# PEER's rows of u: turned by VectorE in 32x32 squares and multiplied as plain fp32, on one core

## What is computed

```python
def peer_ffn(h, q_w, sub_keys, u_tab, v_tab):      # h: 256 x 1024, u_tab and v_tab: 16384 x 1024
    q = (t @ q_w).reshape(n, PEER_H, 2, PEER_DQ // 2)
    s = jnp.einsum('thpd,hpnd->thpn', q, sub_keys)
    s1, i1 = lax.top_k(s[:, :, 0], PEER_TOPK); s2, i2 = lax.top_k(s[:, :, 1], PEER_TOPK)
    ...                                            # the 16 best of the 16 x 16 sums, for each of 8 heads
    gates = jax.nn.softmax(top_s, axis=-1)
    act = jax.nn.gelu(jnp.einsum('chkd,cd->chk', u_tab[i_c], x_c))
    return jnp.einsum('chk,chkd->cd', g_c * act, v_tab[i_c])
```

## Time and profile before

| what | value |
|---|---|
| median of 3 runs | 2324.53 us (2319.58 to 2325.33) |
| the profiled execution: its own time | 2319.86 us |
| its span | 2318.1 us |
| granted clock over the span | 0.966 of full speed |
| busy over the span | PE 2145.5 us (93%), DVE 1409.6 us (61%), ACT 1016.8 us (44%), POOL 186.9 us (8%) |
| HBM | 330.58 MB read, 143 GB/s over the span |

### The profile page before, as it was taken

One profiled execution on the slowest core, in us unless ns is written; L12 is line 12 of the kernel. 1 busy time (PEld: TensorE's weight loads), 2 busy tenths in 40 slices (PEclk: granted clock), 3 DMA queues, 4 the chain that ended last, 5 costly groups with the idle time before them and its releaser, 6 DMA issues.

```text
span 2318.1 us, 37450 instructions
## 1 busy us (share of the span) xinstructions
PE 2145.5 (93%) x14407; PEld 1931.0 (83%) x14407; DVE 1409.6 (61%) x2315; ACT 1016.8 (44%) x1870; POOL 186.9 (8%) x217
## 2 busy tenths in 40 slices
PE   6999899878899999789999699999999999999997
PEld 6876788778788889778888599999999999777775
DVE  5435777677676752154434628997666654666665
ACT  4443443458553343233333424443444444555554
POOL 2101000001000000300000000000223341000000
PEclk9999999999999999879999899999999999999998
DMA  7543566734657743300001333343333335555553
GB/s 254 184 172 110 190 218 220 245 117 160 221 166 267 252 158 131 83 1 1 1 1 37 109 111 128 128 137 119 115 113 114 115 119 175 189 190 190 190 190 136
DMA packets 157432, 333.74 MB, mean 144 GB/s; under 512 B 17382, under 2 KB 69340, under 8 KB 157160
## 3 DMA queue, kind: packets, MB, share of 16 engines
q1 hardware_dynamic: 153896, 321.18, 41.0%
q0 software_dynamic: 3392, 10.52, 1.3%
HBM read 330.58 MB, written 1.08 MB: 143 GB/s over the span
## 4 chain that ended last, share of the span: by engine, by line
PE 73%; DVE 12%; PEld 7%; ACT 3%; issue 3%; SPq 1%; DMA 1%; PEldq 1%; DVEq 0%; ACTq 0%
PE psum L2130 18%; PE psum L2131 17%; PE psum L2132 17%; PE psum L2652 4%; PE psum L2699 2%; PEld psum L2130 2%; PEld psum L2131 2%; PEld psum L2132 2%; DVE weights_lo L1493 2%; PE psum L2542 2%; PE psum L2548 2%; DVE u_lo L2080 1%; PE psum L2523 1%; ACT weights_hi L1037 1%; PE psum L2428 1%
## 5 line engine op out<-in xcount | busy, mean ns | idle before, releaser
L1493 DVE TENSOR_TENSOR weights_lo<-weights,weights_hi 128x1024 fp32r<-128x1024 f32 (+2 forms) x336 | 345.3, 1085 | 260.4 <-ACT weights_hi L1037 255.3
L2130 PE MATMUL psum<-input_hi,weights_hi 128*128 128x256 f32 x1288 | 370.9, 288 | 19.0 <-DVE weights_lo L1493 6.1
L1037 ACT ACTIVATE weights_hi<-weights 128x1024 fp32r<-128x1024 f32 (+2 forms) x336 | 289.2, 931 | 178.7 <-PEq L2177 117.5
L2131 PE MATMUL psum<-input_lo,weights_hi 128*128 128x256 f32 x1288 | 367.1, 285 | 0.0
L2132 PE MATMUL psum<-input_hi,weights_lo 128*128 128x256 f32 x1288 | 366.9, 285 | 0.0
L2130 PE MATMUL psum<-input_hi,u_hi 128*128 128x256 f32 x1024 | 299.8, 293 | 0.0
L2132 PE MATMUL psum<-input_hi,u_lo 128*128 128x256 f32 x1024 | 289.3, 283 | 0.0
L2131 PE MATMUL psum<-input_lo,u_hi 128*128 128x256 f32 x1024 | 289.2, 282 | 0.0
L2130 PEld LDWEIGHTS psum<-input_hi,weights_hi 128*128 128x128 f32 x1288 | 250.0, 194 | 34.6 <-issue 32.7
L2080 DVE TENSOR_TENSOR u_lo<-psum,u_hi 128x512 fp32r<-128x512 f32 x256 | 164.8, 686 | 167.4 <-ACT u_hi L1419 165.9
L2131 PEld LDWEIGHTS psum<-input_lo,weights_hi 128*128 128x128 f32 x1288 | 250.0, 194 | 0.0
(11 more groups left out here) (376 smaller groups left out, 4001.4 us busy)
## 6 DMA issues: line engine op xcount, KB each, us to landing
u_rows<-in_peer_u_dram SPq DMA_DIRECT2D x128, 512.0 KB, 3.4
weights<-in_ffn_w_in_dram SPq DMA_DIRECT2D x44, 1024.0 KB, 7.3
v_rows_even<-in_peer_v_dram SPq DMA_DIRECT2D x64, 512.0 KB, 3.5
v_rows_odd<-in_peer_v_dram SPq DMA_DIRECT2D x64, 512.0 KB, 3.4
weights<-in_ret_w_in_dram SPq DMA_DIRECT2D x24, 1024.0 KB, 7.3
ada_rows_in<-in_ada_w_dram SPq DMA_DIRECT2D x24, 1024.0 KB, 5.2
weights<-in_ffn_w_out_dram SPq DMA_DIRECT2D x44, 512.0 KB, 6.5
weights<-in_lru_w_in_dram SPq DMA_DIRECT2D x12, 1024.0 KB, 6.3
```

The costliest lines, as they stand in the source:

```text
L1037: nc.scalar.activation(whi[:, r, at_], wraw[:, r, at_], ACT.Copy).then_inc(s_whi[r], 1)
L1493: ins = nc.vector.tensor_tensor(wlo[:, r, at_], wraw[:, r, at_], whi[:, r, at_].bitcast(F32), ALU.subtract)
L2130: nc.tensor.matmul(o, ah, bh, start=start, stop=False)
L2131: nc.tensor.matmul(o, ah, bl, start=False, stop=False)
```

## The change

For blocks 0 to 112 ("plain" blocks; PARTED is 113) the rows of u are no longer split. DVE transposes them in 32x32 squares from SBUF to SBUF into one of four buffers, and PE makes 8 plain fp32 products of 256 columns with an input that is not split either (`input_t`, HT, made once by POOL as the sum of hi and lo). A transpose in squares stays inside groups of 32 partitions, so the order of the contraction is changed to fit: row 256a + 32k + j of the contraction goes to partition 32a + j of chunk k. That reaches the load of u (4 DMAs of 32 rows, 1 KB to a partition), the load of the query weights (8 DMAs of 256 KB for a slot instead of 2 of 1 MB), and the second operation of `modulate`, which writes in that order. Blocks 113 to 127 are still split, from the turned rows in SBUF, with one ACT and one DVE operation of 128x1024. The one-hot rows are made by one DVE comparison of 128x1024, and ACT multiplies in the gates with four operations of 128x128.

```diff
+PARTED = GROUP_FIRST + GROUPS
+def plain_buffer(j):
+    return j % 4
+def parted(j):
+    return (j - PARTED) // 2 + 1
...
+        HT = Region("u's hi parts, before", low.at, 8 * KB).take("input_t", [P, KT, S])
+        UF2 = Region("u's lo parts, before", low.at, 8 * KB).take("u_turned_more", [P, 2, KT, P])
+        UT = Region("idle rows", rows_at, 8 * KB).take("u_turned", [P, 2, KT, P])
+        UF = [UT[:, 0], UT[:, 1], UF2[:, 0], UF2[:, 1]]
...
             def load_u(j, i=0):
-                    sp.wait_ge(s_ut[b], i * 2 + 2 * (j // 2))
-                sp.dma_start(UR[:, b, :], u_tab[bass.ds(i * 256 + j * P, P), :]).then_inc(s_ur[b], 16)
+                    sp.wait_ge(s_ut[b], i + j // 2)
+                for c in range(4):
+                    four = u_tab[bass.ds(i * 256 + j * P + c * 32, 32), :].rearrange("e (a k) -> a e k", a=4)
+                    sp.dma_start(UR[:, b, c * 256:(c + 1) * 256], four).then_inc(s_ur[b], 16)
...
+            for j in (2, 3):
+                r, use = slot(SLOTS["peer_q"] + j)
+                pool.wait_ge(s_wlo[r], use + 1)
+            for h in range(2):
+                half = slice(4 * h, 4 * h + 4)
+                nc.gpsimd.tensor_tensor(HT[:, half, :], HH[:, half, :].bitcast(F32), HL[:, half, :].bitcast(F32), ALU.add)\
+                    .then_inc(s_ht, 1)
...
             def u_high(j):
+                if j < PARTED:
+                    return
+                b = j % 2
+                act.wait_ge(s_ut[b], j // 2 + 1)
+                act.wait_ge(s_ap, max(j - 1, PARTED))
+                nc.scalar.activation(UTH[:, b, :, :], UT[:, b, :, :], ACT.Copy).then_inc(s_uh[b], 1)
+
+            def gates_in(g):
+                act.wait_ge(s_oh, g + 1)
+                for x in range(4):
+                    one = ONE[:, g % 2, 0, x, :]
+                    t = 4 * g + x
+                    ins = nc.scalar.activation(one, one, ACT.Copy, scale=HKT[:, 2, t:t + 1])
+                ins.then_inc(s_ohg, 1)
...
+            def turn_u(j):
+                b = j % 2
+                dve.wait_ge(s_ur[b], 64 * (j // 2) + 64)
+                if j < PARTED:
+                    dst = UF[plain_buffer(j)]
+                    if j >= 4:
+                        dve.wait_ge(s_ap, j - 3)
+                else:
+                    dst = UT[:, b]
+                    if j < PARTED + 2:
+                        dve.wait_ge(s_ap, max(m for m in range(j) if m < PARTED and plain_buffer(m) == b) + 1)
+                    else:
+                        dve.wait_ge(s_ul[b], parted(j - 2))
+                nc.vector.transpose(dst.rearrange("p k (c e) -> p c k e", c=4),
+                                    UR[:, b, :].rearrange("p (c k j) -> p c k j", c=4, k=KT)).then_inc(s_ut[b], 1)
+
             def u_low(j):
+                if j == 0:
+                    turn_u(0)
+                if j + 1 < P:
+                    turn_u(j + 1)
+                if j >= PARTED:
+                    b = j % 2
+                    dve.wait_ge(s_uh[b], parted(j))
+                    nc.vector.tensor_tensor(UTL[:, b, :, :], UT[:, b, :, :], UTH[:, b, :, :].bitcast(F32), ALU.subtract)\
                         .then_inc(s_ul[b], 1)
...
             def activations(j):
+                if j < PARTED:
+                    pe.wait_ge(s_ut[b], j // 2 + 1)
+                    for k in range(KT):
+                        ins = nc.tensor.matmul(PS[:, 2 + b, 0:S], UF[plain_buffer(j)][:, k, :], HT[:, k, :],
+                                               start=k == 0, stop=k == KT - 1)
...
             def gates(g):
-                pe.wait_ge(s_oh, g + 1)
+                pe.wait_ge(s_ohg, g + 1)
...
+            pe.wait_ge(s_ht, 2)
-            u_steps(turn_u, activations, beside)
+            u_steps(lambda *a: None, activations, beside)
```

More of the change, by code:

```diff
@@ L355, with slot_loads @@
 GROUP_FIRST = len(PICKS) + 3
+PARTED = GROUP_FIRST + GROUPS
[3 more added lines that the diff above has]
+    return (j - PARTED) // 2 + 1
+def slot_loads(s0, use):
+    late = s0 - SLOTS["peer_q"]
+    return 32 * use + 32 if late < 0 else 32 * (use - late // 2) + 16 * KT * (late // 2 + 1)
 def group_made(j):
@@ L555, in first_and_second_block @@
         NS = Region("idle input", hh_at + 8 * KB, 8 * KB).take("na_scores", [P, 4, 512])
+        NP = Region("idle input", hh_at + 8 * KB, 8 * KB).take("scaled", [P, TT, D])
         NPT = Region("low-rank inputs", lora_at, 4 * KB).take("na_probs_t", [P, 2, 512])
@@ L639, in first_and_second_block @@
         s_oh = sem("s_oh")
+        s_ohg = sem("s_ohg")
+        s_ht = sem("s_ht")
         s_ur = [sem(f"s_ur{b}") for b in range(2)]
@@ L996, in _ @@
             load_rows(14, 18)
+            for u in range(4):
+                evacuated(UNITS["norm_p"] + u)
+            for j in (2, 3):
+                r, use = slot(SLOTS["peer_q"] + j)
+                pool.wait_ge(s_wlo[r], use + 1)
[3 more added lines that the diff above has]
+                    .then_inc(s_ht, 1)
             def gate_block(j):
@@ L1455, in beside @@
                     gates_out(group_made(j - 2), j + 1)
+                if group_made(j) is not None:
+                    gates_in(group_made(j))
             def high(j, i=0):
@@ L1462, in high @@
                     act.wait_ge(s_gm, GROUPS)
+                if j < 2 and isinstance(i, int):
+                    act.wait_ge(s_ul[j], parted(P - 2 + j))
                 if j == 2 and isinstance(i, int):
@@ L1553, in gain_row, with modulate @@
                 return dst
-            def modulate(src, scale):
+            def modulate(src, scale, turned=False):
                 shift = row()
+                lies = (lambda x: x.rearrange("p (a k j) -> p a k j", a=4, k=KT)) if turned else lambda x: x
                 for tt in range(TT):
                     inverse_rms(tt)
-                    chain.done(nc.vector.scalar_tensor_tensor(XS[:, tt, :], src[:, tt, :], rs[:, tt:tt + 1], scale,
+                    scaled = (NP if turned else XS)[:, tt, :]
+                    dst = XS[:, tt, :].rearrange("p (k a j) -> p a k j", a=4, k=KT) if turned else XS[:, tt, :]
+                    chain.done(nc.vector.scalar_tensor_tensor(scaled, src[:, tt, :], rs[:, tt:tt + 1], scale,
                                                               ALU.mult, ALU.mult))
-                    chain.done(nc.vector.tensor_tensor(XS[:, tt, :], XS[:, tt, :], shift, ALU.add))
+                    chain.done(nc.vector.tensor_tensor(dst, lies(scaled), lies(shift), ALU.add))
                     dve.sem_inc(s_xs, 1)
@@ L2007, in _ @@
             dve.wait_ge(s_x, 10)
-            modulate(X, GAIN[1])
+            modulate(X, GAIN[1], True)
             for u in range(4):
@@ L2089, in one_hot_rows @@
                     dve.wait_ge(s_gf, g - 1)
[L2090 to L2095 removed]
+                both = [P, 2, 4, P]
+                iota = IOTA[:, :].unsqueeze(1).unsqueeze(1).broadcast_to(both)
+                places = HKT[:, 0:2, 4 * g:4 * g + 4].unsqueeze(3).broadcast_to(both)
+                nc.vector.tensor_tensor(ONE[:, g % 2], iota, places, ALU.is_equal).then_inc(s_oh, 1)
             def beside(j):
```

48 lines of the change are left out of this document (15 added, 33 removed).

## The result

| | before | after |
|---|---|---|
| median of the runs | 2323.11 us (4 runs, 2319.58 to 2325.33) | 2516.27 us (4 runs, 2506.79 to 2518.94) |
| ratio to before | | 1.0826 (1.0793 to 1.0858) |
| span of the profiled execution | 2318.1 us | 2517.2 us |
| first product of u | 1397.45 us | 1423.0 us |
| first product of v | 1946.90 us | 2145.1 us |

The kernel got 8.3% slower, where I had forecast 1.6% faster (2287 us against 2324.53). The loss at the start of v is 198 us, so all of it arises before that point: 26 us before the first product of u, and 173 us in the u stage.

A forecast was written before the change was run, and what follows sets the result against it. PE and DVE were taken as near their limit in the first 46 blocks, PE alone later. Gains of 9 + 17 + 8 = 34 us from 2319.86 gave 2286, median 2287 us; 8-in-10 range 2266 to 2313.

The forecast's parts named there:

- The loads of u: Four DMAs of 128 KB a block: last piece lands 4 to 5.5 us after its buffer is free, hidden by little.
- Query weights: hidden: Query weight loads had 6 us or more to spare; 8 issues instead of 2 add 3, so no cost.
- Rival 4: Loads of u do not hide: last piece 6.5 us late, 14 us lost, 2301 us; 0.10 together with rival 5.
- A plain block on PE: Eight plain fp32 products take 3.47 us instead of 3.75, gaining 0.27 us a block; with gates 4.37 instead of 4.64.
- The transpose on DVE: DVE's transpose of 1024 elements a partition lasts 1.2 us, the next operation starting 1.13 us after it.
- Rivals 1, 2 and 3: DVE's transpose: slower, 1.4 to 1.7 us (0.13); 1.9 us or more, kernel slower (0.09); fast, 0.6 us, 2266 us (0.07).
- Blocks 0 to 49: First part of the u stage, led by DVE: gain 9 us, two of them from the start.
- Blocks 50 to 112, with gates: PE leads, so its gain arrives whole: 63 blocks x 0.27 = 17 us.
- a stall of 1.6: Ahead of block 113 PE waits some 2.5 us for DVE, of which gates cover 0.90: 1.6 us lost.
- rival 5: Blocks with gates: ACT's new work delays the gates, 6.3 us per 0.1 us beyond cover; 0.10 together with rival 4.
- Block 113 and the end: Last blocks, split without PE transposes: 13 x 0.79 = 10.3 us gained, less 2.5 of stalls, net 8 us.
- The second stall: Block 114 waits for a hi part that ACT makes behind two sets of gate work: 0.9 us.

The follow-up runs named there:

- e3_both_16: Changed kernel with the loads of u and of the query weights both cut by quarters of the partitions, 32 rows slowest: 2289.35 us, ratio to before 0.9862.
- e1: Changed kernel with only the loads of u cut by quarters of the partitions, slowest dimension 32 rows, still four DMAs of 128 KB: 2312.71 us.
- e2: Changed kernel with only the query weights' loads cut by quarters of the partitions, 4 DMAs for a slot instead of 8: 2491.49 us.
- e6: Kernel before with rows of u permuted so that the load's slowest dimension is 4, one DMA of 512 KB a block: 2425.01 us.
- e9: Kernel before with rows of u permuted so that the load's slowest dimension is 2, one DMA of 512 KB a block: 3062.21 us.
- e5: e3_both_16 with split products from block 50 on instead of 113: 2325.45 us, ratio to before 1.0023.
- e5r: e5 with ACT's hi part placed ahead of the gates' work: 2259.39 us, ratio to before 0.9741.
- e8: Kernel before with rows of u permuted so that the load's slowest dimension is 8, one DMA of 512 KB a block: 2331.77 us.

## Why the prediction was wrong

**The step that failed is "The loads of u", and with it "Query weights: hidden".** I priced the new loads by bytes and by count of DMAs: a load lands in 3.4 us, 128 KB in 4.0, so the last piece should land 4 to 5.5 us after its buffer was free, and the term stood at nothing. It took 9.9 us (1799.27 to 1809.15), and the u stage grew by 173 us. Those rows are of loads whose slowest dimension is the partitions. The diff says `"e (a k) -> a e k", a=4`: I read it for what it does to the partitions and not for what it does to the transfer. For the query weights I counted issues only ("8 issues instead of 2 add 3", with "6 us or more to spare"); a slot needs 22 us at 95 GB/s, SP's 32 issues took 2.49 us each at the median, where the 8 issues before took 0.44, and the first product of u came 26 us late. The prediction has two prices for a load, its issue and its delay, and none for its rate, the time for which it keeps its engines: with four engines that is 5.57 us a block, above every price of the other engines.

**Rival 4 had the place and not the mechanism.** It let the last piece land 6.5 us after its buffer was free, as a delay with the ring of two buffers around it, so two blocks in 7.6 us and 14 us in all. By the same formula 9.9 + 1.25 gives 11.1 us for two blocks, 5.57 each, as measured, but that reads the cause backwards: with four packets in flight nearly all the time the rate sets the block, and the 9.9 us follow from it, since each load queues behind the one before. By this reading more buffers would not have helped, which no run tried. A rate of this size (94 GB/s) was not in any row before; to bound it from above I would have had to ask how many engines the new form can use. The range had no such case, so 2516 lay far outside.

**The other steps can be read in e3_both_16**, which has them without the slow loads. Its v stage starts at 1915.75, 31.2 us earlier than before; the forecast said 34.

- *A plain block on PE*: 3.46 us (1800.38 to 1803.84), forecast 3.47; with gates 4.35, forecast 4.37. Right, and the rows of the form itself were the better guide than the 3.93 us estimated against them. The four passes that the Trainium skill's FP8 and Floating Point Precision, TensorE Precision Notes, states are not refuted by it: 3.46 us over 32 passes is 0.108 us a pass, and the estimate had put the 0.123 us of a whole split product in its place.
- *The transpose on DVE*: 1.245 us long and the next operation 1.16 to 1.17 us after its start, forecast 1.2 and 1.13. Right, up to 0.04 too low. Rivals 1, 2 and 3 fall.
- *Blocks 0 to 49*: forecast 9 us. The first gates start at 1595.20, where the kernel before had them at 1602.11: 6.9 us. Blocks with keys take 4.14 us, with picks 3.63, with match 4.90, which is the forecast's 4.13, 3.63 and 4.90, so the transpose's 0.04 is not where the rest went. DVE's start is: its first transpose stands at 1395.14, not 1393.9, and the third (1401.06, shown above) waits 3.55 us for its load, so the first step of the picks begins at 1402.23, where the kernel before had it at 1399.03. The forecast had counted 2 us gained at the start and left out this wait, though its own 4 to 5.5 us for a load in a freed buffer would have given it. From there to the end of the picks DVE has no wait, and PE still waits 1.85 us for them at 1581.00.
- *Blocks 50 to 112, with gates*: forecast 17 us less a stall of 1.6. From the first gates to the last the kernel before took 292.3 us (1602.11 to 1894.42), e3_both_16 275.2 (1595.20 to 1870.43): 17.1 us, the stall of 1.71 ahead of block 113 included, where the forecast comes to 15.4. A block saved 0.29 us and not 0.27, and block 113, which is split, lies inside this stretch. Right in its mechanism, and rival 5 falls in e3_both_16: PE is busy for all of 257 us.
- *Block 113 and the end*: after the last gates 52.5 us before and 45.3 now, 7.2 gained; the forecast had 10.3 - 0.9 = 9.4. The second stall measured 1.08 for my 0.9. Most blocks take 2.94 us, but one 3.99, two 3.3 to 3.4: DVE waits there for ACT's hi part or 1.0 us for the load, as the part on the loads had feared for these blocks.

In the changed kernel itself none of these gains arrive, since the load sets each block, whatever stands in it. That also is why the kinds of blocks, 2.9 to 4.9 us by their own work, nearly all take 5.57.

That the rate is set by the number of engines is shown, by e1, e2, e6 and e9 and by the packets in flight. Why four engines give 24 GB/s each with pieces of 1 KB and 26 with 4 KB, and eight only 15, is not; the packets say only that each takes longer.

## What to carry to other kernels

When a load is rearranged, write down the slowest dimension of both sides and ask how many of the 16 DMA engines it can feed; bytes and count of DMAs don't show it. Here both rearrangements could be cut so that the long dimension came first, into as many or fewer DMAs (e1, e2, e3). Price a load by its delay and, apart from that, by its rate. In a profile a flat number of GB/s with a DMA share near k/16 is the sign, and "0.27 busy" then means saturated. Where several engines wait in a ring and none is full, look for the operation needed first that is queued behind one needed later (e5, e5r: 66 us by one order).

## What the runs showed of the hardware that I had not expected

- Rates of SP's queue here, by the slowest dimension of a load of 512 KB in pieces of 4 KB: 2 gives 53 GB/s, 4 gives 105, 8 about 123. With 16, 141 GB/s were drawn at a share of 0.42, and the load was not the limit. Pieces of 1 KB on 4 engines: 94.
- A DMA on fewer than 16 engines also costs SP more: 547 ns to issue on four, against 333 before and 317 in e3_both_16 for the same 128 KB. A load of 512 KB took 532 ns on two engines (e9), 554 on four (e6) and 621 on eight (e8). Groups of the changed kernel and of e3_both_16:

```profile
L901 SPq DMA_DIRECT2D u_rows<-in_peer_u_dram x512: 522/547/1293, 1410.8 to 2126.2; - x171
```

```profile
L902 SPq DMA_DIRECT2D u_rows<-in_peer_u_dram x512: 316/317/1612, 1384.3 to 1904.5; - x171
```

- The one-hot comparison of 128x1024 on DVE takes 1.18 us in the changed kernel, but in e5r_parted_50_act 1.21 to 1.81, and what goes with it is whether POOL is in the middle of an operation when it starts. From 1595 us on, the 39 that began while POOL did nothing took 1.21 to 1.22 us; of the 24 that began during a POOL operation 20 took 1.56 to 1.81. The lo parts of that run show the same: 1.18 to 1.22 us for the 7 that began without POOL, up to 2.28 for the 58 others. It cuts both ways: POOL's product of 208 columns takes 0.70 us where it begins before DVE's comparison (at 1802.01, 0.13 us ahead), and that of 212 columns 1.70 where it begins 0.02 us after one (1806.02). No run took POOL's work away, so that the two hold each other up is read from these times and not shown by an experiment.
- The sum of hi and lo on POOL, two operations of 1024, takes 2.37 us each, hidden as forecast.
